# Mixture-of-experts pieces of 32 rows in four column groups, with the results stored from ScalarE

## The chip, the cores and the metric

The kernel runs on one core of one Trainium2 chip. The metric is the device time of one execution in microseconds, the median of several. Times of single instructions, waits and transfers come from one profiled execution of the kernel before.

## The reference, cut to what matters

A backbone of two layers works on 256 latent tokens and 256 context tokens of width 1024. Each layer is normalisation, attention, and then a mixture of 16 experts. In the first layer all 512 tokens go through the experts, in the second only the 256 latent ones. All numbers are float32.

```
def _grouped_moe(t, router_w, router_b, w_gate, w_up, w_down):
    scores = jax.nn.sigmoid((t @ router_w).astype(jnp.float32))
    ...
    g_idx = lax.top_k(grp_score, 1)[1][:, 0]          # one of 4 groups of 4 experts
    ...
    e_idx = lax.top_k(jnp.where(in_group, sel, -jnp.inf), TOP_K)[1]   # the best 2 in it
    ...
    for e in range(N_EXPERTS):
        he = jax.nn.silu(t @ w_gate[e]) * (t @ w_up[e])
        y = y + gates[:, e:e + 1] * (he @ w_down[e]).astype(jnp.float32)
```

Each expert holds three weights of 2 MiB: gate and up (1024 x 512) and down (512 x 1024). Every token gives two rows of work, so a layer has 1024 and 512 rows. The reference's own router, on its inputs of seed 0, gives the experts 0 to 15 these rows:

```
layer 0: 104  81  51  90 | 83  42  83 114 | 55  66  72  49 | 42  28  35  29
layer 1:  22  15  31  18 | 30   4  21  45 | 26  16  22  30 | 70  87  38  37
```

## The kernel before, in words

All engines run programs written out by hand, in order, and meet only at semaphores. `ring` is an SBUF buffer of nine slots of 2 MiB. In the expert stage they are three sets of gate, up and down, and expert 3i + a uses set a. SP issues all weight loads.

The router's results decide at run time how many chunks each expert has. VectorE counts rows per expert, works out each token's position (`posidx`) and each chunk's first row (`chunk_row`). GpSimd (POOL) scatters the tokens' normalised rows into the DRAM tensor `h_rows`, sorted by expert, with indirect DMAs. Then the experts run chunk by chunk: POOL loads a chunk's rows of 1024 numbers, PE turns them (`turn_rows`, L574), ACT copies them out of PSUM to `hc_t` (L802, L803), and PE multiplies them with gate and up (L584, `gate_up`). The result is turned (L601), silu and product are applied by ACT (L810, L814) and VectorE (L1181 to L1193), and PE multiplies with down (L611). ACT copies the result to `yrow` (L818, L820) and POOL stores it to the DRAM tensor `y_rows` (L928). After the last chunk POOL gathers the rows of each token back (L939), and they are added to the stream.

A chunk has up to 128 rows in layer 0, or 64 where an expert's last chunk needs no more, and 64 rows in layer 1. A chunk of 64 rows packs two matmuls into the two halves of the array's columns, with 64 columns each: gate and up side by side, or the two halves of down's output. The numbers of chunks follow from the rows above: layer 0 has 16, eight of 128 and eight of 64 rows, and layer 1 has 18 of 64 rows.

When an expert's last chunk is through, a tiny matmul (L618) raises `set_free`, and SP loads the weights of the expert three places on into that set (L302). Experts 0 to 2 are loaded before the stage. There is one buffer for a chunk's rows: the load of chunk g + 1 starts when chunk g's rows are turned. There is one `yrow`: ACT waits for the stores of the chunk before it.

## Time and profile before

| | before |
|---|---|
| median of 3 runs | 1252.38 us (1247.89 to 1255.44) |
| the profiled execution, its own time | 1254.75 us |
| its span, first to last instruction | 1252.9 us |
| mean granted TensorE clock | 0.916 of full speed |
| PE busy | 1048.7 us (84%) |
| DMA traffic | 317.77 MB, mean 254 GB/s |

PE is TensorE's matmul part and PEld its weight loads. SPq, ACTq and POOLq are the sequencers of those engines, where a DMA's issue shows. A float32 matmul shows as two MATMUL instructions. The DMA share is the mean busy share of the 16 DMA engines, and it can read a little over 1. The expert stage of layer 0 lies at about 410 to 707 us, that of layer 1 at about 947 to 1222 us.

### The profile page before, as it was taken

The numbers are of one execution on the slowest core, as the hardware profiler recorded it, in microseconds if no ns is written. First come the engines' busy times: TensorE is split into PE (matmuls) and PEld (weight loads), VectorE is DVE, ScalarE is ACT, GpSimd is POOL, SyncE is SP. The second block draws the span as 40 slices with busy tenths as digits, with TensorE's granted clock in tenths as the row PEclk, the third lists the DMA queues.
The fourth block names the chain that finished last, engine by engine and source line by source line (L and its number), as shares of the span: only waits on it lengthen the run. The fifth ranks groups of instructions, "written<-read, shape, count | busy, mean of one in ns | idle before, by whom it ended". The sixth has DMA issues, their size and how long they took to land.

```text
span 1252.9 us, 16814 instructions
## 1 busy us (share of the span) xinstructions
PE 1048.7 (84%) x5809; PEld 663.6 (53%) x5810; DVE 383.7 (31%) x1019; ACT 360.1 (29%) x766; POOL 86.9 (7%) x145
## 2 busy tenths in 40 slices
PE   4799989988963899999999459988938987787992
PEld 2244654433443677676755356855835555454652
DVE  1356666563144000000011064778160100000112
ACT  3322255552031122122122143267021221221221
POOL 0000000000002001001011110000010110110111
PEclk9899999998965899999999769999967988888996
DMA  9930299797033189999999980050352999999953
GB/s 318 401 151 0 89 387 329 259 362 272 0 134 134 52 308 400 344 399 346 398 348 397 414 315 1 13 207 1 135 201 88 382 378 380 381 379 388 374 171 109
DMA packets 127534, 317.77 MB, mean 254 GB/s; under 512 B 5872, under 2 KB 6144, under 8 KB 127488
## 3 DMA queue, kind: packets, MB, share of 16 engines
q1 hardware_dynamic: 113680, 276.54, 59.3%
q0 software_dynamic: 12096, 40.38, 9.0%
q8 instruction: 30, 0.49, 0.2%
q10 hardware_dynamic: 1712, 0.23, 0.1%
q14 instruction: 16, 0.13, 0.0%
HBM read 296.68 MB, written 19.40 MB: 252 GB/s over the span
## 4 chain that ended last, share of the span: by engine, by line
PE 65%; SPq 11%; DMA 8%; DVE 7%; ACT 4%; issue 3%; POOL 1%; ACTq 1%; POOLq 0%; DVEq 0%
PE bank L584 17%; SPq L302 11%; PE bank L435 9%; PE bank L611 9%; PE bank L535 7%; DMA ring<-in_w_up_dram 4%; PE bank L378 3%; PE bank L505 3%; PE bank L476 2%; PE bank L574 2%; PE bank L488 2%; PE bank L546 1%; PE bank L444 1%; DVE h_t L1010 1%; PE bank L423 1%
## 5 line engine op out<-in xcount | busy, mean ns | idle before, releaser
L584 PE MATMUL bank<-ring,h_t 128*64 128x256 f32 (+1 forms) x2176 | 317.0, 401 | 31.1 <-DMA ring<-in_w_up_dram 28.3
L584 PEld LDWEIGHTS bank<-ring,h_t 128*64 128x64 f32 (+1 forms) x2176 | 232.3, 157 | 104.1 <-issue 44.0
L611 PE MATMUL bank<-ring,h_t 128*64 128x512 f32 (+1 forms) x544 | 151.8, 597 | 17.2 <-DVE h_t L1193 14.6
L435 PE MATMUL bank<-h_t,ring 128*128 128x512 f32 (+1 forms) x320 | 118.4, 525 | 12.3 <-ACT h_t L719 12.3
L1184 DVE COPY h_t<-bank 128x256 f32<-128x256 f32 x52 | 22.1, 424 | 338.7 <-PE bank L584 338.7
L611 PEld LDWEIGHTS bank<-ring,h_t 128*64 128x64 f32 (+1 forms) x544 | 56.5, 149 | 91.2 <-issue 91.2
L435 PEld LDWEIGHTS bank<-h_t,ring 128*128 128x128 f32 x320 | 62.6, 196 | 60.8 <-issue 41.0
L535 PE MATMUL bank<-tokm,ring 128*128 128x512 f32 (+1 forms) x256 | 85.7, 497 | 1.0 <-DVE tokm L1032 1.0
L574 PE MATMUL bank<-cst,h_t 128*128 128x128 f32 x288 | 40.6, 286 | 38.6 <-DMA h_t<-h_rows 38.6
L991 DVE RECIPROCAL work<-work 128x512 f32<-128x512 f32 (+1 forms) x20 | 54.3, 2713 | 59.5 <-ACT work L729 59.5
L1010 DVE TENSOR_REDUCE h_t<-bank 128x1 f32<-128x512 f32 (+1 forms) x96 | 57.3, 597 | 47.8 <-PE bank L476 26.5
L814 ACT ACTIVATE h_t<-bank 128x128 f32<-128x128 f32 x52 | 12.9, 278 | 201.5 <-PE bank L601 201.5
L535 PEld LDWEIGHTS bank<-tokm,ring 128*128 128x128 f32 x256 | 49.4, 194 | 37.7 <-issue 31.8
L779 ACT ACTIVATE h_t<-bank 128x512 f32<-128x512 f32 (+1 forms) x96 | 50.2, 524 | 57.3 <-PE bank L488 30.1
L768 ACT ACTIVATE ring<-bank,h_t 128x512 f32<-128x512 f32 (+1 forms) x96 | 58.5, 610 | 5.3 <-DVE h_t L1015 4.4
L574 PEld LDWEIGHTS bank<-cst,h_t 128*128 128x128 f32 x288 | 32.9, 145 | 49.6 <-issue 48.8
L818 ACT ACTIVATE work<-bank 128x512 f32<-128x512 f32 x34 | 20.3, 597 | 134.6 <-PE bank L611 134.6
L1181 DVE TENSOR_TENSOR h_t<-bank,h_t 128x256 f32<-128x256 f32 x16 | 6.8, 424 | 168.7 <-ACT h_t L810 168.7
L488 PE MATMUL bank<-cst,ring 128*128 128x128 f32 x320 | 50.6, 280 | 8.0 <-DVE ring L1025 6.7
L928 POOL DMA_DIRECT2D y_rows<-work x68 | 37.0, 543 | 197.7 <-issue 196.2
L488 PEld LDWEIGHTS bank<-cst,ring 128*128 128x128 f32 x320 | 35.3, 141 | 27.2 <-DVE ring L1025 20.3
L476 PE MATMUL bank<-ring 64*128 64x128 f32 (+3 forms) x144 | 47.0, 434 | 1.6 <-DMA work<-ring 1.6
(175 smaller groups left out, 1115.6 us busy)
## 6 DMA issues: line engine op xcount, KB each, us to landing
ring<-in_w_gate_dram SPq DMA_DIRECT2D x32, 2048.0 KB, 16.3
ring<-in_w_up_dram SPq DMA_DIRECT2D x32, 2048.0 KB, 22.3
ring<-in_w_down_dram SPq DMA_DIRECT2D x32, 2048.0 KB, 21.8
ring<-in_ada_w_dram SPq DMA_DIRECT2D x24, 2048.0 KB, 10.4
ring<-in_w_in_dram SPq DMA_DIRECT2D x8, 1536.0 KB, 21.9
h_t<-h_rows POOLq DMA_DIRECT2D x18, 512.0 KB, 7.1
ring<-in_w_out_dram SPq DMA_DIRECT2D x4, 2048.0 KB, 10.5
y_rows<-work POOLq DMA_DIRECT2D x52, 128.0 KB, 5.3
```

Source lines behind the costliest of these rows:

```text
L302: sp.dma_start(slot(s, k), src).then_inc(ew_in[l][s], 16)
L435: last = mm(bank[1 + i % 2][:, 0:widths[i]], qk_weights(i, k), h_t[:, k, 0:widths[i]], start=(k == 0), stop=(k == KD - 1))
L476: last = mm(o[:, c0:c1], q_t, k_t[:, c0:c1], start=True, stop=(c0, c1) != masked)
L488: last = turn(bank[4 + n % 2][:, P * q:P * q + P], probs[:, n % 4, P * q:P * q + P], ident)
L535: last = mm(bank[4 + m % 2][:, 0:P * nt], wout[k // 4][:, k % 4, P * m:P * m + P], y_t[:, k, 0:P * nt], start=(k == 0), stop=(k == KD - 1))
L574: last = turn(bank[5 + k // 4][:, P * (k % 4):P * (k % 4) + P], hc[:, P * k:P * k + P], ident)
L584: last = mm(o, hc_t[:, k, 0:rows], w[s][:, k, 256 * half:256 * half + 256], start=(k == 0), stop=(k == KD - 1))
L611: last = mm(o, he_t[:, k, 0:rows], wd[:, k, 512 * n:512 * n + 512], start=(k == 0), stop=(k == KF - 1))
L768: do(probs[:, n % 4, 0:kn], bank[n % 4][:, 0:kn], ACT.Exp, bias=negmax[:, n:n + 1], scale=SCALE, accum_out=lsum[:, n:n + 1]).then_inc(exp_ ...
L779: do(probs_t[:, 0:nk, col:col + P], bank[4 + n % 2][:, 0:P * nk].rearrange("p (k q) -> p k q", k=nk), ACT.Identity).then_inc(pt_ready, 1)
L991: v.reciprocal(rstd[:, 0:n], rstd[:, 0:n])
L1010: link(v.tensor_reduce(smx[:, n:n + 1], bank[n % 4][:, 0:keys(tt)[1]], AX.X, ALU.max))
```

## The change

The experts work on pieces of 32 rows in both layers, and every expert has at least two pieces (`LEAST`), empty ones included. A piece's matmuls use four column groups of 32: for each of 8 slices of the contraction, four matmuls of 256 columns (gate and up, two halves each), and for each of 4 slices four quarters of down's output. The rows of each expert start at a multiple of 32 in `h_rows` and `y_rows`, with gaps between, so piece g is rows 32g to 32g + 31 and `chunk_row` is gone. SP fills both tensors with zeros (from a block of zeros in `table`) early in the program. A piece is loaded as 128 partitions of 256 numbers, two pieces ahead, into two buffers `hc_got`; VectorE copies it to `hc`, and after PE's two transposes to `hc_t`. The down product of piece g - 1 stands behind gate and up of piece g. ACT itself issues four stores of 32 KB for each piece. Gate and up slots are refilled when the last gate and up product of their expert is done, and the down slot when its last down product is done. In the route step the piece counts now come before `posidx`.

In the diff the removed functions of PE, ACT and POOL are left out where they are shown above; "..." marks every cut.

```diff
-SHORT = P // 2
-CHUNK = [P, SHORT]
-MAXCH = TOK_TILES[0] * P // CHUNK[0]
-MAX_CHUNKS = [NE + 2 * t * P // n for t, n in zip(TOK_TILES, CHUNK)]
-GT = max(MAX_CHUNKS) + 2
-ROWS = 2 * (SEQ + CTX)
+CHUNK = 32
+MAXCH = TOK_TILES[0] * P // CHUNK
+LEAST = [2, 2]
+MAX_CHUNKS = [n * NE + 2 * t * P // CHUNK for n, t in zip(LEAST, TOK_TILES)]
+ROWS = P * -(-CHUNK * (max(MAX_CHUNKS) + 3) // P)
...
+        hc_got = hflat[:, 0:512]
+        hc = hflat[:, 1280:1536]
+        hc_t = hflat[:, 512:768].rearrange("p (k r) -> p k r", k=KD)
+        he = hflat[:, 768:1024]
+        act_g = hflat[:, 1024:1152].rearrange("p (j m) -> p j m", j=2)
+        he_t = hflat[:, 1152:1280].rearrange("p (j m) -> p j m", j=2)
+        pos = work[:, 736:744]
+        yrow = work[:, 0:256]
...
+            def refill(l, e, a):
+                done = end_of(sp, l, e)
+                sp.wait_ge(gu_mm[l], done)
+                load_expert(l, e + 3, a, (0, 1))
+                sp.wait_ge(down_mm[l], done)
+                load_expert(l, e + 3, a, (2,))
...
+                    for rows_dram in (h_rows, y_rows):
+                        sp.dma_start(rows_dram[:, :].rearrange("(n p) d -> p n d", p=P),
+                                     table[:, C_Z:C_ALL].unsqueeze(1).to_broadcast([P, ROWS // P, D])
+                                     ).then_inc(rows_zeroed, 16)
...
-                with sp.Fori(1, 5) as i:
+                sp.wait_ge(route_ready, l + 1)
+                with sp.Fori(0, 4) as i:
                     for a in range(3):
-                        sp.wait_ge(set_free[l][a], i)
-                        load_expert(l, 3 * i + a, a)
-                sp.wait_ge(set_free[l][0], 5)
-                load_expert(l, 15, 0)
+                        refill(l, 3 * i + a, a)
+                refill(l, 12, 0)
...
             def experts(l):
                 def turn_rows(n):
 
...
+                    pe.wait_ge(hc_moved[l], n + 1)
+                    for j in range(2):
+                        last = turn(bank[5][:, P * j:P * j + P], hc[:, P * j:P * j + P], ident)
+                    last.then_inc(hc_turned[l], 1)
+                def gate_up(g, a):
+                    w = [ring[:, 3 * a + s, :].rearrange("p (k n) -> p k n", k=KD) for s in range(2)]
+                    pe.wait_ge(hc_ready[l], g + 1)
                     for k in range(KD):
...
+                        for q in range(4):
+                            last = mm(bank[1][CHUNK * q:CHUNK * q + CHUNK, 0:256], hc_t[:, k, :],
+                                      w[q // 2][:, k, 256 * (q % 2):256 * (q % 2) + 256],
+                                      start=(k == 0), stop=(k == KD - 1))
                     last.then_inc(gu_mm[l], 1)
 
...
+                def turn_he(g):
+                    pe.wait_ge(he_ready[l], g + 1)
+                    for j in range(2):
+                        last = turn(turned_he[:, j, :], he[:, P * j:P * j + P], ident)
+                    last.then_inc(he_turned[l], 1)
+                def down(g, a):
                     wd = ring[:, 3 * a + 2, :].rearrange("p (k n) -> p k n", k=KF)
...
+                    pe.wait_ge(het_ready[l], g + 1)
                     pe.wait_ge(rows_ready[l], g + 1)
                     for k in range(KF):
...
+                        h = he_t[:, k % 2, CHUNK * (k // 2):CHUNK * (k // 2) + CHUNK]
+                        for q in range(4):
+                            last = mm(bank[4][CHUNK * q:CHUNK * q + CHUNK, 0:256], h,
+                                      wd[:, k, 256 * q:256 * q + 256], start=(k == 0), stop=(k == KF - 1))
                     last.then_inc(down_mm[l], 1)
 
...
+                def weights_in(a, turns, parts):
+                    for part in parts:
+                        pe.wait_ge(ew_in[l][3 * a + part], 16 * turns)
+                def expert_long(e, a, turns, prev):
+                    g0, g1 = first_of(pe, l, e), end_of(pe, l, e)
+                    weights_in(a, turns, (0, 1))
+                    gate_up(g0, a)
+                    turn_rows(g0 + 1)
+                    if prev is not None:
+                        down(g0 - 1, prev)
+                    weights_in(a, turns, (2,))
+                    turn_he(g0)
+                    with pe.Fori(g0 + 1, g1) as g:
+                        gate_up(g, a)
+                        turn_rows(g + 1)
+                        down(g - 1, a)
+                        turn_he(g)
...
+                expert = expert_long if LEAST[l] > 1 else expert_short
                 pe.wait_ge(route_ready, l + 1)
                 turn_rows(0)
+                expert(0, 0, 1, None)
                 with pe.Fori(0, 5) as i:
...
+                    expert(3 * i + 1, 1, i + 1, 0)
+                    expert(3 * i + 2, 2, i + 1, 1)
+                    expert(3 * i + 3, 0, i + 2, 2)
+                if LEAST[l] > 1:
+                    down(all_chunks(pe, l) - 1, 0)
...
             def experts(l):
...
+                act.wait_ge(route_ready, l + 1)
+                act.wait_ge(rows_zeroed, 32)
+                with act.Fori(0, all_chunks(act, l)) as g:
+                    act.wait_ge(he_turned[l], g + 1)
+                    do(act_g, turned_he[:, :, 0:2 * CHUNK], ACT.Silu).then_inc(silu_done[l], 1)
                     act.wait_ge(down_mm[l], g + 1)
...
+                    act.wait_ge(rows_stored[l], 64 * g + 64)
+                    do(yrow, bank[4][:, 0:256], ACT.Identity).then_inc(rows_ready[l], 1)
+                    act.wait_ge(rows_ready[l], g + 2)
+                    for q in range(4):
+                        act.dma_start(y_rows[bass.ds(CHUNK * g, CHUNK), 256 * q:256 * q + 256],
+                                      yrow[CHUNK * q:CHUNK * q + CHUNK, :]).then_inc(rows_stored[l], 16)
...
+                def load_rows(n, i):
+                    pool.dma_start(hc_got[:, 256 * i:256 * i + 256],
+                                   h_rows[bass.ds(CHUNK * n, CHUNK), :].rearrange("r (q c) -> (r q) c", q=4)
+                                   ).then_inc(hc_in[l][i], 16)
+                load_rows(0, 0)
+                load_rows(1, 1)
+                total = all_chunks(pool, l)
+                with pool.Fori(0, (total + 1) // 2) as m:
+                    for i in range(2):
+                        pool.wait_ge(hc_moved[l], 2 * m + 1 + i)
+                        load_rows(2 * m + 2 + i, i)
+                pool.wait_ge(hc_in[l][0], (total + 3) // 2 * 16)
+                pool.wait_ge(hc_in[l][1], (total + 3) // 2 * 16)
+                pool.wait_ge(hc_moved[l], total + 2)
+                pool.wait_ge(rows_stored[l], total * 64 + 64)
...
+                link(v.scalar_tensor_tensor(out=cmp3, in0=cst[:, C_G + 1:C_G + MAXCH].unsqueeze(1).to_broadcast([P, NE, MAXCH - 1]),
+                                            scalar=rows, in1=tot.unsqueeze(2).to_broadcast([P, NE, MAXCH - 1]),
+                                            op0=ALU.mult, op1=ALU.is_lt))
+                link(v.tensor_reduce(nch, cmp3, AX.X, ALU.add))
+                link(v.tensor_scalar(nch, nch, float(LEAST[l] - 1), 1.0, ALU.max, ALU.add))
+                link(v.tensor_tensor(tri3, nch.unsqueeze(1).to_broadcast([P, NE + 1, NE]), fe, ALU.mult))
+                link(v.tensor_reduce(firstf, tri3, AX.X, ALU.add))
+                v.tensor_copy(first[:, :], firstf).then_inc(route_ready, 1)
+                link(v.scalar_tensor_tensor(out=te(rank), in0=firstf[:, 0:NE].unsqueeze(1).to_broadcast([P, nt, NE]),
+                                            scalar=rows, in1=te(rank), op0=ALU.mult, op1=ALU.add))
...
+                def rows_turned(n):
+                    dve.wait_ge(hc_turned[l], n + 1)
+                    v.tensor_copy(hc_t.rearrange("p (q j) r -> p j q r", j=2),
+                                  bank[5][:, 0:256].rearrange("p (j r q) -> p j q r", j=2, q=4)).then_inc(hc_ready[l], 1)
+                def rows_in(n):
+                    dve.wait_ge(hc_in[l][0], (n + 2) // 2 * 16)
+                    if not isinstance(n, int) or n > 0:
+                        dve.wait_ge(hc_in[l][1], (n + 1) // 2 * 16)
+                    v.tensor_copy(hc, hc_got[:, bass.ds(n % 2 * 256, 256)]).then_inc(hc_moved[l], 1)
+                rows_in(0)
+                rows_turned(0)
+                rows_in(1)
+                with dve.Fori(0, all_chunks(dve, l)) as g:
+                    dve.wait_ge(gu_mm[l], g + 1)
+                    v.tensor_copy(he, bank[1][:, 0:256]).then_inc(he_ready[l], 1)
+                    rows_turned(g + 1)
+                    dve.wait_ge(silu_done[l], g + 1)
+                    v.tensor_tensor(he_t, act_g, turned_he[:, :, 2 * CHUNK:P], ALU.mult).then_inc(het_ready[l], 1)
+                    rows_in(g + 2)
```

PE, the expert stage of layer 0. Before, one chunk of 64 rows (L584 gate and up, L574 turn the next rows, L601 turn the hidden values, L611 down):

```order
L584 MATMUL bank<-ring,h_t 64x256 [waits ew_in0_4,ew_in0_3]
L584 MATMUL bank<-ring,h_t 64x256 x31
L574 MATMUL bank<-cst,h_t 128x128 [waits hc_in0]
L574 MATMUL bank<-cst,h_t 128x128 x7
...
L601 MATMUL bank<-cst,h_t 128x128 [waits he_ready0]
L601 MATMUL bank<-cst,h_t 128x128
...
L611 MATMUL bank<-ring,h_t 64x512 [waits het_ready0,rows_ready0,ew_in0_5]
L611 MATMUL bank<-ring,h_t 64x512 x3
L611 MATMUL bank<-ring,h_t 64x512 [waits het_ready0]
L611 MATMUL bank<-ring,h_t 64x512 x3
```

Of the change, the loop over the second and later pieces (L572 gate and up, L563 turn rows, L592 down of the piece before, L581 turn the hidden values):

```order
L572 MATMUL bank<-ring,h_t 32x256 [waits hc_ready0]
L572 MATMUL bank<-ring,h_t 32x256 x31
...
L563 MATMUL bank<-cst,h_t 128x128 [waits hc_moved0]
L563 MATMUL bank<-cst,h_t 128x128
L592 MATMUL bank<-ring,h_t 32x256 [waits rows_ready0,het_ready0]
L592 MATMUL bank<-ring,h_t 32x256 x15
L581 MATMUL bank<-cst,h_t 128x128 [waits he_ready0]
L581 MATMUL bank<-cst,h_t 128x128
```

The down product has moved behind the next piece's gate and up, and the turning of the hidden values now comes last.

ACT, the loop body of the expert stage in layer 0. Before, for a chunk of 64 rows (L814 silu, L802 and L803 the next rows, L818 the result):

```order
L814 ACT_TABLE_LOAD
L814 ACTIVATE h_t<-bank 128x128 [waits he_turned0]
...
L802 ACTIVATE h_t<-bank 128x512 [waits hc_turned0]
L803 ACTIVATE h_t<-bank 128x512
...
L817 ISA [waits down_mm0]
L818 ACTIVATE work<-bank 128x512 [waits rows_stored0]
```

Of the change, one piece (L817 silu, L820 the result, L823 the stores):

```order
L817 ACT_TABLE_LOAD
L817 ACTIVATE h_t<-bank 128x128 [waits he_turned0]
L819 ISA [waits down_mm0]
L820 ACTIVATE work<-bank 128x256 [waits rows_stored0]
...
L823 ISA [waits rows_ready0]
L823 DMA y_rows<-work 32x256
L823 ISA
L823 DMA y_rows<-work 32x256
L823 ISA
L823 DMA y_rows<-work 32x256
L823 ISA
L823 DMA y_rows<-work 32x256
```

The copies of the next rows have left ACT for VectorE. Four DMA issues have come, and they stand ahead of the next turn's table load and silu.

## Rows read from the trace of the kernel before

**Rows 1.** The page: DMA share in 40 equal slices of the span, in tenths.
```profile
DMA  9930299797033189999999980050352999999953
```
**Rows 2.** The chain that ended last, layer 0's expert stage: start, duration, what.
```profile
413.26 15.85 PE bank L584 x64
...
666.13 26.08 DMA ring<-in_w_up_dram
692.35 8.81 PE bank L584 x64
703.18 3.67 PE bank L611 x16
```
**Rows 3.** The same chain, layer 1's expert stage.
```profile
947.17 9.88 PE bank L584 x64
...
1143.36 9.08 PE bank L584 x64
...
1218.77 3.67 PE bank L611 x16
```
**Rows 4.** Timeline of SP's issues: the first refill of layer 0 and of layer 1.
```profile
438.23 0.39 SPq L302 DMA_DIRECT2D ring<-in_w_gate_dram  x1
...
963.25 0.38 SPq L302 DMA_DIRECT2D ring<-in_w_gate_dram  x1
```
**Rows 5.** Windows in layer 1, and early in the program; the last three numbers are PEclk, DMA share, GB/s.
```profile
970.00:980.00 10.00, 9.44 (x70) 5.53 (x70) 1.18 (x4) 3.35 (x6) 1.60 (x3) 1.00 1.05 371
1200.00:1210.00 10.00, 9.44 (x70) 5.32 (x67) 1.35 (x4) 1.98 (x5) 1.49 (x3) 1.00 0.35 114
60.00:80.00 20.00, 20.00 (x50) 9.31 (x49) 8.56 (x7) 4.31 (x8) 0.00 (x0) 1.00 0.76 287
80.00:145.00 65.00, 65.00 (x186) 35.05 (x186) 42.19 (x44) 14.33 (x23) 0.00 (x0) 1.00 0.00 0
```
**Rows 6.** Timeline of a 64-row chunk in layer 0: start, duration, what, idle before.
```profile
460.80 7.13 PE L584 MATMUL bank<-ring,h_t 128*64 128x256 f32 x64
467.86 1.10 PE L574 MATMUL bank<-cst,h_t 128*128 128x128 f32 x8
468.79 0.60 PE L601 MATMUL bank<-cst,h_t 128*128 128x128 f32 x4
469.20 0.50 ACT L814 ACTIVATE h_t<-bank 128x128 f32<-128x128 f32 x2 [4.32 <-PE bank L601]
469.52 0.51 DVE L1193 TENSOR_TENSOR h_t<-h_t,bank 128x128 f32<-128x128 f32 x2 [1.12 <-ACT h_t L814]
469.95 3.65 PE L611 MATMUL bank<-ring,h_t 128*64 128x512 f32 x16 [0.56 <-DVE h_t L1193]
```
**Rows 7.** Timeline: matmuls of four column groups of 512 columns, adaLN weights.
```profile
33.50 1.90 PE L378 MATMUL bank<-ring,scv 128*2 128x512 f32 x16
```
**Rows 8.** Timeline, layer 1: ACT copies the result, then loads silu's table.
```profile
1209.49 0.60 ACT L818 ACTIVATE work<-bank 128x512 f32<-128x512 f32 x1 [3.04 <-PE bank L611]
...
1210.11 1.28 ACT L814 ACT_TABLE_LOAD   x1
```
**Rows 9.** Groups by line and form: an ACT copy of 256 columns.
```profile
L810 ACT ACTIVATE h_t<-bank 128x256 f32<-128x256 f32 x14 | 5.4, 384 | 68.7 <-PE bank L584 68.7
```
**Rows 10.** One line each: POOL's stores, POOL's row loads, issue to landing min/median/max.
```profile
DMA to landing us min/median/max: 2.2/5.4/7.6
...
DMA to landing us min/median/max: 3.3/6.6/8.6
```
**Rows 11.** Timeline of ACT's own DMA issues at the program's start.
```profile
2.47 1.09 ACTq L842 DMA_DIRECT2D h_t<-in_c_dram  x1
3.59 0.28 ACTq L842 DMA_DIRECT2D h_t<-in_c_ctx_dram  x1
```
**Rows 12.** The chain between the scatter and the first chunk of layer 0.
```profile
400.19 4.52 DMA h_rows<-tokm,posidx
406.24 3.52 DMA h_t<-h_rows
```

240 lines of the change are left out of this document (42 added, 198 removed).

## The prediction
> **What bounds the kernel now.** I read the page's time slices first. The DMA engines are busy for 80% or more of slices 15 to 24 (438 us on) and 90% or more of 32 to 38 (971 us on), the two expert stages [rows 1]; everything the change does to the steady work lies there. Then the chain. In layer 0 it starts on PE, with the first gate and up product at 413.3 us, and ends on the loads: the last expert's up weight is in flight from 666.1 and lands at 692.2. PE ends the stage at 706.85 (703.18 + 3.67) [rows 2]. So layer 0 is PE's for most of the stage and the loads' at its end. In layer 1 the loads bound the middle. Expert 12's up weight is what PE waits for until 1143.4. From there PE has six chunks of 64 rows to do and ends at 1222.4 [rows 3]. The windows say the same: full DMA share from 970 on, and 0.35 in the window from 1200 [rows 5], so the last weight lands at about 1203. The refills begin at 963.25 [rows 4], which makes (1203 - 963.25) / 13 = 18.5 us for one expert's weights with its rows.
>
> **How many pieces.** Each expert has its rows divided by 32, rounded up, and at least 2. The rows listed above give 42 pieces in layer 0 (4 3 2 3, 3 2 3 4, 2 3 3 2, 2 2 2 2) and 34 in layer 1 (twelve times 2, then 3 3 2 2). A chunk of 64 rows took about 13.1 us of PE (1143.36 to 1222.44 for six, rows 3); two pieces have to be measured against that.
>
> **A piece on PE.** Gate and up took 7.13 us for 64 rows over two column groups. The number of matmuls stays, four run together instead of two: 3.5 us. The down product: 3.65 us becomes 1.8. Two transposes of rows instead of eight in 1.10 us: 0.3. Two of hidden values instead of four in 0.60 us: 0.3 [all rows 6]. That is 5.9, and I take 6.0 for a piece bound by PE. That four column groups run together the trace shows at 512 columns: 16 instructions in 1.90 us [rows 7], where two groups of the same length need 3.65 [rows 6].
>
> The Trainium skill speaks against that: "TensorE: Matmul & The Clock Gate", section "Measured speedup vs the span model": three column tiles gave 2.38x instead of 3x. By it 3.5 + 1.8 us would be 6.7, a piece 7.3 us, and the sum about 1256 us. The row above has no such loss, but it has 512 columns and not 256. A rival below takes it up.
>
> **A piece on ACT.** The order listing shows the loop: silu, wait for the down product, copy the result, four DMA issues, table load, next silu. From the end of the down product of piece g - 1 to that of piece g:
> - PE's semaphore 0.13, the copy of 256 columns 0.38 [rows 9], its semaphore and registers 0.15;
> - four issues. Without company one took 0.28 us, and one took 1.09 [rows 11]; I take 0.42 with its register step: 1.7;
> - loop and branch 0.25, the table load 1.28 [rows 8], silu 0.28, semaphore 0.05, VectorE's product 0.29 (0.51 for two that overlap, rows 6), semaphore 0.1;
> - the down product itself 1.8.
>
> The sum is 6.4 us. It is above PE's 6.0, so ACT, not PE, would set the pace: the silu of a piece stands behind the stores of the one before.
>
> **The store's round trip.** There is one `yrow`. The copy of piece g's result waits until all four stores of piece g - 1 have landed. The last of them is issued 1.8 us after the copy began (0.38 + 0.15 + three issues), so a piece cannot be shorter than about 1.8 us plus its landing. No row shows a store from ACT. The nearest are POOL's, two a chunk, of 128 or 256 KB: 2.2 us at least, 5.4 in the median, 7.6 at most [rows 10]. So a piece takes between 6.4 (landing up to 4.6) and 9.4 us. POOL spends part of its time on making the descriptors, and layer 0's DMA would be slightly less than full; I take 4.9 us, which is nearest to the median, and a piece of 6.7 us.
>
> The page "DMA: Bandwidth & Descriptors", section "Queues, rings and completion order", of the Trainium skill says that each DMA engine goes round between the queues at packet granularity. By it ACT's small stores would wait for one packet of SP's and land near the minimum, which gives pieces of 6.4 us. POOL's median of 5.4 against 2.2 speaks against it.
>
> **Loads of rows.** The load of a piece is issued some two pieces ahead of its use, 13 us, and POOL's loads landed in 3.3 to 8.6 us [rows 10]. Hidden; with one buffer only it would cost up to 2 us a piece. VectorE has four short operations in a piece, under 2 us of 6.7: hidden.
>
> **Layer 0.** The start of the first product moves little. Later come four operations ahead of `posidx`, 0.2 to 0.45 us each, +1.4. Earlier: no register load of `chunk_row` between the scatter's landing at 404.7 and the load at 406.2 [rows 12], -1.2; a load of a quarter of the bytes, two transposes instead of eight and one short copy instead of two long ones, against VectorE's extra copy, -1.5. So the first product starts at 412.0. PE's clock is at half there: 64 rows took 9.88 us where a later chunk took 7.13 [rows 3, 6], so I add 1.9. The end is then 413.9 + 42 x 6.7 = 695.3 us against 706.85: **-11.5 us**. The loads set a floor: first refill at 413.9 + 3 x 6.7 + 3.5 = 437.5, hardly before today's 438.2 [rows 4]. Thirteen experts at 18.5 us end at 678, the last up weight lands some 6 us before, and two pieces and a down product follow it: 686. At 6.4 us a piece this floor binds: -21.
>
> **Layer 1.** The start is 1.3 us earlier as well: 945.9, 947.4 with the slow clock. Gate and up slots come free after the second gate and up product, at 947.4 + 6.7 + 3.5 = 957.6 instead of 963.25. As the loads set the pace until expert 12, its up weight lands 5.7 us earlier, at 1137.7. Then come ten pieces: 1139.7 + 10 x 6.7 = 1206.7. The last up weight at about 1192, two pieces and a down product give 1208. The later one counts: **-14 us**.
>
> **The rest.** The zeros are 17.8 MB. SP reaches them at about 72 us, and between 80 and 145 us the DMA engines do nothing [rows 5]. At the 371 GB/s of a full window [rows 5] they need 48 us: hidden. At half that rate they would end at 168 us and meet the next loads from 145 on; that costs 0 to 5 us, and I take 0. After the last down product four issues of ACT replace POOL's two, no difference that I can price above 1 us.
>
> **Sum.** 1254.75 - 11.5 - 14 = 1229.3 us for the profiled execution. That one lies 2.4 us above the median of the runs shown, so I predict **1227 us**.
>
> **The rivals.** Both layers together (413.9 + 42 P - 706.85, and 1139.7 + 10 P - 1222.4) give 52 P - 375.6 us for P between 7 and 9, so it breaks even at P = 7.2 us a piece. A change of 0.5%, 6.3 us, is about what a measurement of this kernel can tell; that is P = 7.1 and P = 7.35.
> - *The forecast*: P of 6.5 to 7.1, 1216 to 1246 us. For it: both loops on ACT come out there. Chance 0.38.
> - *Stores land early*, P up to 6.5. Then the loads bind both layers: -21 and -15, 1215 us. Even P = 6.0 would give no more. For it: ACT needs no descriptors made by software. Against: POOL's median. Chance 0.25.
> - *No difference*, P of 7.1 to 7.35, by landings of 5.4 us: 1246 to 1259. Chance 0.09.
> - *A fourth column group has to wait* (slower): the two products take 4/3 of 5.3 us, and P is 7.8 on PE: +30, 1282 us. Against: the four groups of rows 7. Chance 0.04. The Trainium skill's figure above is the same in a milder form.
> - *Stores land late* (slower). With one `yrow`, each microsecond over 5.5 costs 42 us in layer 0 and 10 in layer 1, and the chain has no slack. At a landing of 6.2 us P is 8.0: 52 x 8 - 375.6 = +40, 1292 us. It decides from P = 7.35 on. For it: the maximum of 7.6. Against: as PE slows down the queue gets shorter. Chance 0.12.
> - *ACT's issues stand behind SP's* (slower). The up weight of rows 2 took 26 us from issue to landing, so SP's queue is full of work, and one issue of ACT took 1.09 us where the next took 0.28 [rows 11], both soon after SP's first loads. If a store waits for one issue of SP's, P is 10 to 12: +170 in layer 0 and +100 in layer 1 at 11, about 1520 us. For it that one row alone, of a moment when the queues were far from full. Chance 0.12.
>
> **Chances and range.** Faster: 0.38 + 0.25 = 0.63. Same: 0.09. Slower: 0.12 + 0.12 + 0.04 = 0.28. The range reaches down to 1208, the early stores with 7 us for the errors of the start and the zeros. Up it takes in no difference and the late stores to P of 7.5: 1266 us. What is left out is most of the late stores' far part, the blocked issues, the fourth group, and little below: 0.2.
>
> **What would show it.** In the profile after: a gate and up group of 64 instructions in 3.5 us; the time from one piece to the next 6.4 to 7.0 us in layer 0; the wait ahead of the down product named by VectorE's product or by ACT's copy; ACT's wait ahead of the copy ended by the DMA `y_rows<-work` for part of the pieces; SP's first refill of layer 1 at about 957. If ACT's issues show more than 0.6 us each, or the stores land later than 5.5 us, the prediction is wrong on the high side. If the DMA share in layer 0 is full from 440 on and PE waits for weights, it is wrong on the low side.

## The result: slower by 0.8%, and the profile after

The changed kernel took 1260.87 us (median of 9 runs, 1255.25 to 1265.37), the kernel before 1250.1 us (9 runs, 1247.61 to 1255.44). The ratio is 1.0079, 95% interval 1.0056 to 1.0101. The forecast was 1227 us and faster; the range of 1208 to 1266 holds the time. The profiled execution after has a time of its own of 1258.0 and a span of 1256.3 us.

First the page of the changed kernel: the DMA slices that answer to [rows 1], and the groups of the expert loop.

```profile
DMA  9999498887033389896999944041332999999932
...
L1157 DVE TENSOR_TENSOR h_t<-h_t,bank 128x128 f32<-128x128 f32 x76 | 21.9, 288 | 436.9 <-ACT h_t L817 436.9
...
L817 ACT ACT_TABLE_LOAD x76 | 97.5, 1283 | 180.4 <-issue 170.8
L563 PE MATMUL bank<-cst,h_t 128*128 128x128 f32 x156 | 34.6, 304 | 122.2 <-DVE h_t L1147 122.2
...
y_rows<-work ACTq DMA_DIRECT2D x304, 32.0 KB, 4.7
```

76 pieces ran, 42 and 34, as counted. PE idles 122 us over all pieces ahead of L563, the turn of the *next* piece's rows, until VectorE has copied those rows (L1147), an instruction that had no term in the forecast. The chain that ended last shows a whole piece in layer 0 (start, duration, what):

```profile
503.73 0.39 ACT work L820
504.14 0.05 ACTq L823
504.28 0.32 ACTq L823
504.63 0.04 ACTq L823
504.76 0.32 ACTq L823
505.23 0.32 ACTq L823
505.71 0.32 ACTq L823
...
506.35 1.28 ACT L817
507.65 0.29 ACT h_t L817
507.95 0.12 DVE h_t L1157
...
508.44 0.30 DVE h_t L1147
...
508.79 0.44 PE bank L563 x2
509.23 1.91 PE bank L592 x32
...
511.24 0.39 ACT work L820
```

From copy to copy it is 7.51 us. Two thirds of the pieces of both layers take just that, none takes less, and the others take up to 9.8 (the median pitch of ACT's copies is 7.51 in layer 0 and 7.52 in layer 1). Read it as one loop through three engines, ACT, VectorE and PE: the result's copy, four issues at a pitch of 0.48, the table load, silu, VectorE's product, *then the rows copy behind it*, then PE's turn of the rows, and only behind that the down product. Gate and up lie beside this chain. The timeline has them, and the answer to [rows 6]:

```profile
503.88 3.66 PE L572 MATMUL bank<-ring,h_t 128*32 128x256 f32 x64
...
508.79 0.44 PE L563 MATMUL bank<-cst,h_t 128*128 128x128 f32 x2 [1.25 <-DVE h_t L1147]
...
509.15 1.93 PE L592 MATMUL bank<-ring,h_t 128*32 128x256 f32 x32
```

3.66 us where 7.13 stood, 1.93 where 3.65 stood: four column groups run together at 256 columns too. In the kernel before, a chunk of 128 rows shows what the same 64 matmuls take in one group:

```profile
437.89 14.06 PE L584 MATMUL bank<-ring,h_t 128*128 128x256 f32 x64
```

The windows that answer to [rows 5]:

```profile
970.00:980.00 10.00, 8.80 (x144) 4.66 (x138) 2.09 (x6) 1.95 (x3) 0.70 (x2) 1.00 0.70 240
1200.00:1210.00 10.00, 8.07 (x130) 4.44 (x134) 2.78 (x8) 1.94 (x3) 1.09 (x2) 1.00 0.15 49
60.00:80.00 20.00, 20.00 (x51) 9.50 (x50) 10.15 (x10) 4.94 (x9) 0.00 (x0) 1.00 1.03 384
80.00:145.00 65.00, 63.97 (x188) 35.34 (x186) 40.71 (x41) 14.09 (x23) 2.29 (x4) 1.00 0.71 231
```

From 970 us on the DMA share is 0.70 where it was 1.05: in layer 1 too the pieces set the pace now, and PE waits for the up weights 2.9 us in all, where it was 25.3. The zeros are issued at 56 and 64 us and have landed by 129, and nothing waits for them. Where the time went, by the profiled executions: until layer 0's first gate and up product 413.3 became 406.1 (-7.2); layer 0's experts 293.5 became 324.7 (+31.2); from there to layer 1's first product 240.3 became 230.3 (-10.0); layer 1's experts 275.2 became 266.8 (-8.4); the tail 30.5 became 28.4 (-2.1). These give +3.5 against +10.8 in the medians: before's profiled execution lay 4.7 us over its median, after's 2.9 under, so 7.5 us of the five terms are scatter. The -7.2 at the start is partly scatter and partly two stores that the change dropped, as the last experiment shows.

### The profile page after: what moved, and what is told of

Its sections match the earlier page's. It is cut to its first block, busy times and chain, and to the rows that moved or that the text cites. A ratio compares the mean times of both kernels' runs of the same rounds, so it can differ in the third digit from the quotient of the medians.

```text
span 1256.3 us, 26129 instructions
## 1 busy us (share of the span) xinstructions
PE 1002.4 (80%) x10205; PEld 571.0 (45%) x10206; DVE 436.0 (35%) x1168; ACT 384.4 (31%) x777; POOL 71.7 (6%) x116
## 4 chain that ended last, share of the span: by engine, by line
PE 40%; ACT 12%; ACTq 9%; DMA 9%; issue 7%; DVE 6%; SPq 2%; POOL 1%; DVEq 1%; POOLq 0%
PE bank L592 10%; ACTq L823 9%; PE bank L524 7%; ACT L817 6%; DMA y_rows<-work 4%; PE bank L424 3%; PE bank L494 3%; PE bank L367 3%; PE bank L465 3%; ACT work L820 2%; PE bank L563 2%; PE bank L477 2%; DMA ring<-in_w_up_dram 2%; PE bank L572 2%; SPq L280 2%
## 5 line engine op out<-in xcount | busy, mean ns | idle before, releaser
L572 PE MATMUL bank<-ring,h_t 128*32 128x256 f32 x4864 | 282.1, 384 | 12.5 <-issue 6.4
L572 PEld LDWEIGHTS bank<-ring,h_t 128*32 128x32 f32 x4864 | 153.4, 111 | 120.0 <-issue 28.9
L1157 DVE TENSOR_TENSOR h_t<-h_t,bank 128x128 f32<-128x128 f32 x76 | 21.9, 288 | 436.9 <-ACT h_t L817 436.9
L592 PE MATMUL bank<-ring,h_t 128*32 128x256 f32 x2432 | 150.0, 388 | 10.2 <-DVE h_t L1157 10.2
L563 PE MATMUL bank<-cst,h_t 128*128 128x128 f32 x156 | 34.6, 304 | 122.2 <-DVE h_t L1147 122.2
L424 PE MATMUL bank<-h_t,ring 128*128 128x512 f32 (+1 forms) x320 | 117.6, 523 | 12.3 <-ACT h_t L732 12.3
L820 ACT ACTIVATE work<-bank 128x256 f32<-128x256 f32 x76 | 29.2, 384 | 262.3 <-PE bank L592 229.4
L592 PEld LDWEIGHTS bank<-ring,h_t 128*32 128x32 f32 x2432 | 72.1, 111 | 64.0 <-issue 15.2
L563 PEld LDWEIGHTS bank<-cst,h_t 128*128 128x128 f32 x156 | 15.8, 142 | 158.5 <-DVE h_t L1147 119.3
L907 POOL DMA_DIRECT2D h_t<-h_rows x80 | 43.9, 549 | 528.2 <-DVE h_t L1147 520.8
L465 PE MATMUL bank<-work,ring 64*128 64x128 f32 (+3 forms) x144 | 47.6, 439 | 0.0
```

The lines of the kernel that those rows point to most:

```text
L424: last = mm(bank[1 + i % 2][:, 0:widths[i]], qk_weights(i, k), h_t[:, k, 0:widths[i]], start=(k == 0), stop=(k == KD - 1))
L465: last = mm(o[:, c0:c1], q_t, k_t[:, c0:c1], start=True, stop=(c0, c1) != masked)
L563: last = turn(bank[5][:, P * j:P * j + P], hc[:, P * j:P * j + P], ident)
L572: last = mm(bank[1][CHUNK * q:CHUNK * q + CHUNK, 0:256], hc_t[:, k, :], w[q // 2][:, k, 256 * (q % 2):256 * (q % 2) + 256], start=(k == 0) ...
L592: last = mm(bank[4][CHUNK * q:CHUNK * q + CHUNK, 0:256], h, wd[:, k, 256 * q:256 * q + 256], start=(k == 0), stop=(k == KF - 1))
L820: do(yrow, bank[4][:, 0:256], ACT.Identity).then_inc(rows_ready[l], 1)
```

## The experiments

Edits are against the changed kernel unless said. The times, with the chief numbers that were read from each trace (layer 0 and 1: from the first gate and up product to the last down product; pitch: median of ACT's copies in layer 0; wait: what ACT's copy in layer 0 waited for the stores, from the groups by line):

| kernel | us | ratio to before, 95% | layer 0 | layer 1 | pitch | wait |
|---|---|---|---|---|---|---|
| before | 1250.1 | | 293.5 | 275.2 | | |
| changed | 1260.87 | 1.0056 to 1.0101 | 324.7 | 266.8 | 7.51 | 22 |
| rows_first | 1234.8 | 0.9845 to 0.9894 | 310.2 | 259.0 | 7.10 | 87 |
| table_out | 1222.04 | 0.9744 to 0.9791 | 295.5 | 260.3 | 6.87 | 135 |
| two_yrow | 1223.51 | 0.9765 to 0.9808 | 297.4 | 260.2 | 6.1 and 7.6 | 0 |
| quarter_stores | 1185.89 | 0.9456 to 0.9513 | 271.4 | 246.7 | 6.19 | 14 |
| one_store | 1350.42 | 1.0795 to 1.0831 | 373.2 | 312.4 | 9.41 | 182 |
| silu_first | 1195.16 | 0.9554 to 0.9598 | 270.2 | 252.0 | 6.27 | 0 |
| silu_one_buffer | 1216.78 | 0.9691 to 0.9760 | 298.4 | 251.7 | 6.91 | 247 |
| no_lag | 1240.74 | 0.9919 to 0.9952 | 315.7 | 260.0 | 7.10 | 16 |
| no_lag_two | 1240.92 | 0.9907 to 0.9957 | 315.4 | 260.0 | 7.18 | 0 |
| pool_stores | 1595.92 | 1.2723 to 1.2803 | 507.9 | 416.8 | 12.8 | |
| before_refill | 1232.96 | 0.9864 to 0.9897 | 285.3 | 265.5 | | |
| late_refill | 1280.97 | 1.0211 to 1.0267 | 335.7 | 278.1 | 7.52 | |
| silu_late_refill | 1210.63 | 0.9659 to 0.9720 | 278.4 | 261.2 | 6.27 | |
| with_pads | 1262.39 | 1.0076 to 1.0129 | 329.5 | 266.1 | | |

### Is the chain the bound? Four single edits

**rows_first.**

```diff
+                    rows_in(g + 2)
                     dve.wait_ge(silu_done[l], g + 1)
                     v.tensor_tensor(he_t, act_g, ...).then_inc(het_ready[l], 1)
-                    rows_in(g + 2)
```

> VectorE copies the rows of piece g+2 before it waits for piece g's silu, instead of behind the product. Three theories of the 7.51 us that a piece takes in the changed kernel. T1, one serial chain (down, ACT's copy, four store issues, table load, silu, product, rows copy, turn of the rows, down): the rows copy and the turn leave it, 0.85 us, so 6.7 us a piece, layer 0's expert stage from 325 to about 293 us, layer 1's (34 pieces, near its weight traffic) some 8 us shorter, 1220 us in all (1212 to 1232). T2, TensorE itself at four column groups sets the pace: no change, 1258 to 1263. T3, the round trip of the one result buffer (issue to landing 4.7 us, and ACT's 2.3) sets it: no more than 5 us gained.

Measured: 1234.8 us, 26 under the changed kernel. The chain theory has its mark: the shortest pieces now take 6.65 us, 0.86 less. But only some pieces are short, and most of the 15 us that are missing against the expectation are a new wait. The group of ACT's copy in layer 0, of the changed kernel and then of this one:

```profile
L820 ACT ACTIVATE work<-bank 128x256 f32<-128x256 f32 x42 | 16.1, 384 | 144.3 <-PE bank L592 122.2 <-DMA y_rows<-work 22.1
```
```profile
L820 ACT ACTIVATE work<-bank 128x256 f32<-128x256 f32 x42 | 16.1, 383 | 128.4 <-DMA y_rows<-work 87.1 <-PE bank L592 41.3
```

The copy used to wait for the down product; now it waits for the stores of the piece before. The first limit hid a second one just under it.

**table_out.** A silu of one element ahead of ACT's loop; the trace then has one table load ahead of the loop in each layer, two in all, and none in its body.

```diff
+                do(work[0:1, 0:1], eps[0:1, 0:1], ACT.Silu)
                 with act.Fori(0, all_chunks(act, l)) as g:
```

> A silu of one element stands ahead of ACT's loop over the pieces, so that the loop's body no longer begins with a table load of 1.28 us. T1: the load stands on the chain, so a piece falls from 7.51 us to what is next: 6.2 us by the chain alone, 6.5 us by TensorE's own sum (3.66 + 0.44 + 1.93 + 0.44), 6.8 us by the round trip of the result buffer. I take 6.7: 1218 us in all (1208 to 1230). T2: no change. T3: at most 5 us gained.

Measured: 1222.04 us, 4 over the expected 1218 and within its range. The shortest piece takes 6.23 us (7.51 - 1.28), as the chain says, the median piece 6.87, and the wait for the stores is 135 us (below). The load was never needed a second time: the traces show no load ahead of ACT's copies, and silu runs from turn to turn without one here. It stood in the loop because the loop began without silu's table. The Trainium skill ("ScalarE activation tables: per-element evaluation and per-set limits", section "Table sets in the compiler and the runtime") says that table loads are placed per block; the trace agrees, if the body of the loop is a block: entered without silu's table it has a load in each turn, 76 in all, and entered with it none.

```profile
L821 ACT ACTIVATE work<-bank 128x256 f32<-128x256 f32 x42 | 16.1, 384 | 168.0 <-DMA y_rows<-work 135.0 <-PE bank L592 33.0
```

**two_yrow.** `yrow` becomes two buffers with a semaphore each, and ACT's loop takes two pieces a turn.

```diff
-        yrow = work[:, 0:256]
+        yrow = [work[:, 256 * i:256 * i + 256] for i in range(2)]
...
-                with act.Fori(0, all_chunks(act, l)) as g:
+                with act.Fori(0, all_chunks(act, l) // 2) as m:
+                    for i in range(2):
```

> Two result buffers with a count each; ACT's loop runs over pairs of pieces, so that it has one table load for two pieces instead of two. Two effects are in it. T1: the buffer alone is worth 4 to 5 us (the stretched pieces of layer 0), the halved table loads 0.64 us a piece, 27 us in layer 0: 6.9 us a piece on the mean (7.5 and 6.3 in turn), 1226 us in all (1218 to 1236). T2: no change. T3, the round trip sets the pace: it falls to TensorE's 6.5 us in every piece alike, 1215 us.

Measured: 1223.51 us. In layer 0 the pitch alternates, 6.1 and 7.6 us, as the chain with a table load in every second piece says; a round trip would have shortened all pieces alike.

**quarter_stores.** `for q in range(4)` of the stores becomes `range(1)`; three quarters of the result rows are left out.

> Only the first of the four stores of each piece is issued; the other three quarters of the result rows are left out. T1: three issues at a pitch of 0.48 us leave the chain, 1.4 us, so 6.2 to 6.5 us a piece (TensorE's sum is 6.5), 1210 us in all (1200 to 1222). T2: no change. T3: no more than the shorter landing gives, 1250 or more; T4, the traffic of the stores sets it: also below 1215, but the time then is not in ACT's issues.

Measured: 1185.89 us, lower than expected: pieces go down to 6.19 us, which is PE's own sum (gate and up 3.66, down 1.93, and 0.30 for each pair of transposes, most of whose 0.44 lies beside them), not the 6.5 that I had added up. All four results exclude that the column groups set the pace. This one leaves open whether issues, round trip or traffic was worth it; the next two tell. Its layer 1 can't be compared exactly: with three quarters of the rows missing the router there sees other numbers, and the trace has 33 pieces instead of 34, one piece of some 6 us less.

### One big store, or the stores off the chain

**one_store.**

```diff
-                    for q in range(4):
-                        act.dma_start(y_rows[bass.ds(CHUNK * g, CHUNK), 256 * q:256 * q + 256], yrow[CHUNK * q:...
+                    act.dma_start(y_rows[bass.ds(CHUNK * g, CHUNK), :].rearrange("r (q c) -> q r c", q=4), yrow)
```

> The four stores of a piece's result become one of 128 KB with the same bytes and the same rows of 1 KB. It tells apart why leaving three stores out was worth 75 us. T1, the issues: three issues of 0.48 us leave the chain here too, and the buffer's round trip is as much shorter, so 6.2 to 6.4 us a piece as there (6.19), layer 0's stage about 265 us: 1200 us in all (1190 to 1212). T4, the traffic of the stores beside the weights: nothing of it is gone, so no more than 15 us under the changed kernel, 1245 or more.

Measured: 1350.42 us, a plain miss, in the other direction. The timeline of the stretch beside 500 us:

```profile
500.27 0.55 ACTq L822 DMA_DIRECT2D y_rows<-work  x1
...
501.15 1.28 ACT L817 ACT_TABLE_LOAD   x1 [1.05 <-issue]
...
509.30 0.39 ACT L820 ACTIVATE work<-bank 128x256 f32<-128x256 f32 x1 [6.58 <-DMA y_rows<-work]
```

The issue is as cheap as hoped, but the buffer came free 9.0 us after it. The median of layer 0's 27 waits is 9.2 us. With four stores of 32 KB each lands 4.7 us (median, at most 6.0) after its own issue, and the buffer is free 6.4 us after the first issue (median of the 38 waits of silu_one_buffer below). So the same bytes in one store take some 3 us longer, and with one buffer all of it is paid. Why was not tried, but the counts of DMA packets differ, in the changed kernel and then here:

```profile
DMA packets 142097, 329.37 MB, mean 262 GB/s; under 512 B 10320, under 2 KB 20320, under 8 KB 142048
```
```profile
DMA packets 137537, 329.35 MB, mean 244 GB/s; under 512 B 5760, under 2 KB 15760, under 8 KB 137488
```

All 4560 missing packets are small, 60 for each of 76 pieces. The trace has 32 packets of 1 KB and 16 of 4 bytes for a store of 32 KB, and 128 of 1 KB and only 4 of 4 bytes for the store of 128 KB. If each 4-byte packet stands for one DMA engine that took part, the one store went over 4 engines and each small one over 16. That would explain the longer time; it is argued from the counts, not shown.

**silu_first.** The whole traffic, nothing of it in the chain: two buffers as above, `rows_in(g + 2)` first as above, and ACT's loop in another order, with the first silu ahead of it.

```diff
+                silu(1)
+                with act.Fori(0, half - 1) as m:
+                    for i in range(2):
+                        result(down_mm, 2 * m + 1 + i, m + 1, i)
+                        silu(2 * m + 2 + i)
+                        store(2 * m + 1 + i, i)
```

> Two result buffers, the silu of the next piece ahead of the stores in ACT's loop (its first one stands ahead of the loop, and the table load with it), and VectorE's rows copy ahead of its wait for silu. All four stores stay. T1: nothing of ACT is left between two down products but a copy of 0.38 us, so TensorE sets the pace, 6.19 us as with one store of four: layer 0's stage 42 x 6.2 = 260 us, 65 less than in the changed kernel; layer 1 comes down to its weight traffic, some 10 less: 1188 us (1180 to 1200). T4, traffic: no better than 1215.

Measured: 1195.16 us, 4.2% faster than the kernel before (ratio 0.9576). The timeline shows the period that the change could have had:

```profile
505.34 0.38 ACT L827 ACTIVATE work<-bank 128x256 f32<-128x256 f32 x1 [5.76 <-PE bank L593]
505.49 3.66 PE L573 MATMUL bank<-ring,h_t 128*32 128x256 f32 x64
505.62 0.27 ACT L822 ACTIVATE h_t<-bank 128x128 f32<-128x128 f32 x1
505.90 1.80 ACTq L832 DMA_DIRECT2D y_rows<-work  x4
505.92 0.29 DVE L1181 TENSOR_TENSOR h_t<-h_t,bank 128x128 f32<-128x128 f32 x1 [1.78 <-ACT h_t L822]
...
509.45 1.93 PE L593 MATMUL bank<-ring,h_t 128*32 128x256 f32 x32
```

VectorE's product is done at 506.2 and the down product that needs it starts at 509.45, so PE waits for nobody: it is the bound, in layer 0. In layer 1 PE stands between its own pace and the loads': pieces of 6.3 us alternate with waits for weights (what waited, for what: us in all, times, longest).

```profile
PE bank L573 <- DMA ring<-in_w_up_dram: 25.6, 7, 5.4
```

Stores of 32 KB and their traffic cost nothing that layer 0 shows once nothing waits behind them: its stage takes 270.2 us here and 271.4 with three quarters of them gone. In all it is 1195 us against 1186, where one piece less in layer 1 of quarter_stores is most of the 9 us.

**silu_one_buffer.** The same with one `yrow`.

> The fastest version (silu of the next piece ahead of the stores, table load ahead of the loop, rows copy ahead of the wait for silu) with one result buffer, as in the changed kernel. The order alone leaves TensorE's 6.19 us a piece. If the round trip of the one buffer is the second limit, which the growing wait for the stores says (22 us in layer 0 of the changed kernel, 87 with the rows copy moved, 135 with the table load out): copy 0.4, silu 0.3, issues 2.0, landing 4.7 or less from the last issue, about 6.9 us on the mean as with the table load out, 1222 us in all (1214 to 1230). If the wait was only the place where slack of the rest shows: 1197 (1193 to 1202).

Measured: 1216.78 us. The second buffer is worth 22 us, and nearly all of the wait is the stores':

```profile
L826 ACT ACTIVATE work<-bank 128x256 f32<-128x256 f32 x42 | 16.1, 383 | 268.7 <-DMA y_rows<-work 246.6 <-PE bank L592 22.1
```

So the round trip of one buffer is a limit of its own, 6.9 us a piece. My 6.7 us was this limit, 0.2 too small; the chain stood above it.

### The down product one piece later

**no_lag.** PE's order alone: the expert's loop of the changed kernel's other form, in which the down product follows its own piece.

```diff
-                expert = expert_long if LEAST[l] > 1 else expert_short
+                expert = expert_short
...
-                if LEAST[l] > 1:
-                    down(all_chunks(pe, l) - 1, 0)
```

> TensorE's order of one piece undone: the down product follows its own piece's transposes, and is not one piece later. The list for TensorE: gate and up 3.66, turn of the rows 0.44, turn of the product 0.44, then silu 0.28, VectorE's product 0.29 and the steps between them some 0.2, down 1.93: 7.25 us, with the stores and the table load (4.2 us from the end of down) beside gate and up of the next piece. T1: 7.3 us a piece, held up to 7.5 by the result buffer's round trip, so about as long as with the later down, 1254 us (1246 to 1264): the later down bought nothing here. The rival, by which the later down did hide silu and its product: slower by 1 us a piece, 1300 us.

Measured: 1240.74 us, 20 us *faster* than the changed kernel, where I had expected 7, and below the range. The timeline:

```profile
502.64 0.38 ACT L818 ACTIVATE work<-bank 128x256 f32<-128x256 f32 x1 [2.49 <-PE bank L592]
503.19 1.75 ACTq L821 DMA_DIRECT2D y_rows<-work  x4
505.26 1.28 ACT L815 ACT_TABLE_LOAD   x1 [2.24 <-issue]
...
506.49 0.44 PE L581 MATMUL bank<-cst,h_t 128*128 128x128 f32 x2 [0.17 <-DVE h_t L1152]
506.97 0.28 ACT L815 ACTIVATE h_t<-bank 128x128 f32<-128x128 f32 x1 [0.42 <-PE bank L581]
507.28 0.29 DVE L1155 TENSOR_TENSOR h_t<-h_t,bank 128x128 f32<-128x128 f32 x1 [0.49 <-ACT h_t L815]
...
507.67 1.93 PE L592 MATMUL bank<-ring,h_t 128*32 128x256 f32 x32 [0.73 <-issue]
```

Stores and table load (503.19 to 506.54) now lie beside gate and up; what is left between is 7.1 us. Where the expert changes, PE's register work stands ahead of gate and up without cover, in the row below 1.10 us, for a mean of 7.45 us a piece; with the later down product most of it was hidden.

```profile
495.19 3.66 PE L572 MATMUL bank<-ring,h_t 128*32 128x256 f32 x64 [1.10 <-issue]
```

The layer also starts its pipe sooner: its first result is copied 10.3 us after the first product, instead of 12.3.

**no_lag_two.** The same with the two result buffers of two_yrow.

> TensorE's order undone as in the run without the later down product, and the two result buffers as well, so that no piece waits for the stores. Does the later down product win anything once ACT's stores are off the chain? T1: without it a piece is TensorE's serial list with the bubbles for silu and product, 7.1 us as measured in the free pieces of that run, now in all pieces, so some 5 us under its 1241 in layer 0 and little in layer 1 (which stands near its weight traffic): 1234 us (1228 to 1240). With the later down product and ACT's order mended a piece was 6.19 to 6.27 us and 1195 us in all: so the later product is worth 40 us there, and cost 20 us where the stores stood in its chain. The rival, that the later down product is worth nothing and the ACT order did it all: 1200.

Measured: 1240.92 us, no difference from no_lag, though the 16 us of waiting for the stores are gone: they had lain beside PE's chain. The free piece stays at 7.0 to 7.2 us. So with ACT's order mended the later down product is worth some 45 us (1195 against 1241), and with the stores in its chain it costs 20. The 45 are argued in part: no run has PE's order undone and ACT's mended. But in the rows above silu starts 0.04 us after the turn of the product ends, so ACT's order isn't what PE waits for there. The rival of no worth is out.

### Who issues the stores

**pool_stores.** The four stores move from ACT's loop to POOL's, behind `load_rows`, and behind a wait for the result.

```diff
                         load_rows(2 * m + 2 + i, i)
+                        pool.wait_ge(rows_ready[l], 2 * m + 2 + i)
+                        for q in range(4):
+                            pool.dma_start(y_rows[bass.ds(2 * CHUNK * m + CHUNK * i, CHUNK), 256 * q:256 * q + 256], ...
```

> The stores of the changed kernel are issued by GpSimd again, behind its row load. T1: four issues leave ACT's chain (2 us), but there is still one result buffer, and its round trip becomes copy 0.4, a row load's issue 0.5, four issues 2.2, landing 5.3 or more: 8.4 us or more a piece, where it stood at 7.5. Layer 0's stage 42 x 8.5 = 357 us, layer 1's 290: 1315 us in all (1290 to 1340). The rival, that ACT's issue time is all that matters: 6.3 us a piece, 1200.

Measured: 1595.92 us, 335 us over the changed kernel where 54 were expected. The round trip was not what did it:

```profile
505.44 2.25 POOL L920 DMA_DIRECT2D y_rows<-work  x4 [10.62 <-ACT work L824]
508.21 0.56 POOL L907 DMA_DIRECT2D h_t<-h_rows  x1 [0.52 <-issue]
513.34 0.29 DVE L1151 COPY h_t<-h_t 128x256 f32 x1 [8.02 <-DMA h_t<-h_rows]
513.69 0.69 PE L563 MATMUL bank<-cst,h_t 128*128 128x128 f32 x2 [5.47 <-DVE h_t L1151]
...
514.31 3.62 PE L592 MATMUL bank<-ring,h_t 128*32 128x256 f32 x32
```

POOL waits 10.6 us for a result, and the row load that the next result needs stands behind that wait in its queue: load, copy, turn, down product, result, stores, load: 13.7 us from this result to the next, 12.8 in the median. PE idles between and its clock falls: the down product takes 3.62 us instead of 1.93 (granted clock 0.53 from 514.3 to 518.0 and 0.74 from 500 to 514, where the changed kernel has 0.99 over its layer 0). The run prices my order of POOL's work, not stores by POOL as such; what it shows is what stands in the queue behind a moved wait.

### The refill by parts, and the pads

**before_refill.** The kernel before with this one part of the change: `refill` waits for `gu_mm` and loads gate and up, then for `down_mm` and loads down; `set_free` and its tiny matmul are gone.

> The kernel before with one part of the change: gate and up weights are refilled as soon as their expert's last gate/up product is done, down weights after its last down product, instead of the three after it. In the kernel before the weights of L0 and L1 start late by a down product and the ones product (some 5 to 8 us an expert, where the queue is not full). If this refill is what won layer 1 its 8.5 us: faster by 6 to 8 us, 1243 us (1238 to 1250). If layer 1's gain came from the pieces: no change, 1250.

Measured: 1232.96 us, 15.4 us less than its own runs of before, twice the expectation: 8.2 us in layer 0 and 9.7 us in layer 1 by the profiles. These two lie 27 us apart, 12 more than the medians, so the split is rough. Layer 1's first refill is issued 9.7 us after the first product (941.07 against 931.4), not 16.1 [rows 4].

**late_refill.** The same part undone in the changed kernel.

```diff
-                sp.wait_ge(gu_mm[l], done)
-                load_expert(l, e + 3, a, (0, 1))
                 sp.wait_ge(down_mm[l], done)
-                load_expert(l, e + 3, a, (2,))
+                load_expert(l, e + 3, a)
```

> The changed kernel with the refill by parts undone: an expert's gate and up weights are loaded over only when its last down product is done, which in this order is one piece after its last gate and up. With 7.5 us a piece layer 0 needs 325 us for weights that take some 254, so it hides there: 0 to 4. Layer 1 (34 pieces, 267 us) stands near its traffic: each refill starts 5.6 us later, and where the ring is the bound it is paid: 8 to 20 us. In all 1272 (1262 to 1285). If the refill by parts brought layer 1's gain, most of the 8.5 us that layer 1 was shorter than in the kernel before come back here; if not, 1261.

Measured: 1280.97 us, 20 us more than the changed kernel, where 11 were expected: 11 in each layer by the profile. In layer 1 PE's waits for `in_w_up` grow from 2.9 to 11.1 us; in layer 0 no wait for weights is named, so that half is not explained by a row (its window from 440 to 500 us has a granted clock of 0.91). Some of it may be scatter: layer 0 takes 329.5 us in with_pads, whose expert stage is that of the changed kernel with 324.7.

**silu_late_refill.** The same undone in the fastest version.

> The fastest version with all three weights of an expert loaded over only after its last down product. In the changed kernel that cost 20 us, half of it in each layer. With pieces of 6.2 us TensorE asks for the weights faster (layer 0's 42 pieces in 260 us, the traffic some 250), so late refills are paid in both layers: 20 us or more again, 1220 us (1212 to 1235). The rival, that the refill matters only beside slow pieces: 1200 or less.

Measured: 1210.63 us, 15.5 more than silu_first and just under the range. The refill is worth 15 to 20 us at each of the three paces tried.

**with_pads.** The kernel before stores two pads of 512 KB of zeros behind `h_rows` and `y_rows` at its start. The change drops them, and its description doesn't name that. Here they and ACT's wait for them are put back.

> The changed kernel with the two stores of 512 KB of zeros and ACT's wait for them put back, as in the kernel before. The first stretch of the changed kernel's profile was 3.6 us shorter than that of before. If that is the stores' doing: 1264.5 us (1262.5 to 1266). If it is scatter between profiled executions: 1261.

Measured: 1262.39 us, 1.5 over the changed kernel with intervals that overlap: the time alone shows no effect. The traces show one. PE's first instruction, in the changed kernel and then here:

```profile
11.30 0.39 PE L660 MATMUL bank<-cst,h_t 96*128 96x96 f32 x1 [11.30 <-DMA h_t<-in_table_dram]
```
```profile
14.63 0.40 PE L662 MATMUL bank<-cst,h_t 96*128 96x96 f32 x1 [14.63 <-DMA h_t<-in_table_dram]
```

PE starts at 14.6 to 14.9 us in the three profiles with the pads (before, before_refill, with_pads) and at 11.3 to 11.7 in the 13 without. Layer 0's first product stands at 407.0, 407.4 and 413.3 us with them, and at 401.9 to 407.1 without. So of the 7.2 us by which the changed kernel's profile started layer 0 earlier, some 3 are the pads' and the rest is scatter. Whether they reach the total, 1.5 us can't tell.

## Why the prediction was wrong

I forecast 23 us less than before and measured 11 us more. **The step that failed** is the one of the loads of rows: "VectorE has four short operations in a piece, under 2 us of 6.7: hidden". The sum of an engine's work was small; its place was not. The rows copy stands behind VectorE's wait for silu, the turn of the rows that needs it stands ahead of the down product on PE, and so both joined the chain that I had listed under "a piece on ACT". That list gave 6.4 us; the trace has 7.51, 0.85 of it the rows copy with its registers and the turn, the rest small terms (four issues to the table load 2.07 us from the first issue's start, where I had 1.7 + 0.25; down 1.93 against 1.8). Moving the copy alone took 0.86 us from the free pieces and 26 us from the kernel. The forecast's own formula, 52 P - 375.6, gives +15 us at P = 7.51. That the range holds the time is luck: its upper part stood there for stores that land late, and they landed as taken.

**Right:** the number of pieces; gate and up 3.66 (3.5 forecast) and down 1.93 (1.8); ACT's loop above PE, with the table load in it; the landing of ACT's stores (4.7 us, 4.9 taken); that a round trip of the one buffer is a limit near there (6.9 us by silu_one_buffer, 6.7 taken); the hidden zeros; the sign of each rival: the fourth group does not wait, ACT's issues of 0.32 us do not stand behind SP's (three of 304 took over 1 us, the longest 1.79), the stores do not land late, nor near their least of 1.5 us.

**Layer 0:** -11.5 forecast, +24 at its end (706.85 became 730.87), which is 42 pieces at 0.8 us more than taken, 34 us. **Layer 1:** -14 forecast, its stage -8.4: with pieces of 7.5 us the formula gives -7.6. That agreement is luck in part: the formula lets the loads set the pace up to expert 12, and in this profile the pieces do it throughout, with 2.9 us of waits for the up weights. The refill gave the gain: its first issue stood 10.8 us after the first product (971.97) instead of 16.1, and late_refill gives 11 us of layer 1 back. **The start:** -1.3 forecast, with no term for the dropped pads, and -7.2 in the profiles. **Between the layers** I had priced nothing and the profile has -10.0. All kernels with the change's pieces take 230 to 237 us there, where before takes 240.3 and before_refill 238.6. Which part of the change shortens it was not tried. The pace of layer 0 does not settle it: 237.1 us follow the 270.2 of silu_first, but 235.6 follow the 507.9 of pool_stores.

**The parts of the change, as the runs price them:** refill by parts -15 (in the kernel before) and -20 (in the changed one); the later down product +20 as made, about -45 with ACT's order mended; one result buffer instead of two +22 in the mended version; the rows copy's place +26; the table load in the loop +39 (which is not additive with the rows copy, since the round trip catches both). Pieces, column groups and refill were good for 1217 us with the one buffer and 1195 us with a second; the places of silu, the table load and the rows copy made it 1261.

## What to carry to other kernels

Moving a product one step later doesn't take a chain away, it picks another one: write out, for each engine and in program order, what stands ahead of the next down product, with the waits of *other* engines' instructions that stand behind it, and add that up around the loop. An engine that is 35% busy can still hold the loop, by one 0.3 us copy behind the wrong wait. Stores belong behind whatever the next step waits for, and where a loop's first function has its table not loaded on the way in, the loop pays the load every turn: one instance of the function ahead of the loop took 1.28 us from the shortest pieces. When one limit is lifted, look at what the same instruction waits for next (here 22, 87, 135, 247 us for the stores) before the gain is promised.

## What the runs showed of the hardware that was not expected

- One store of 128 KB over 128 partitions freed its buffer 9.2 us after its issue (median), four of 32 KB 6.4 us after the first issue, with the same packets of 1 KB. The one has 4 small packets of 4 bytes, the four have 64.
- ACT's four issues cost 0.32 us each at a pitch of 0.48, beside a DMA share of 0.85 to 0.93 in layer 0; their landing was 1.5 to 6.0 us.
- Four column groups of 32 rows run 64 matmuls of 256 columns in 3.66 us, against 7.13 for the same number over two groups of 64 and 14.06 in one of 128: hardly a loss from the fourth group. The Trainium skill's 2.38x for three column tiles ("TensorE: Matmul & The Clock Gate", section "Measured speedup vs the span model") does not hold for this shape: going from two groups to four gave 1.95x (7.13 / 3.66), and from one to four 3.84x.
- In pool_stores the same 32 down matmuls took 3.62 us instead of 1.93, which is the clock's lower level (1.2 instead of 2.4 GHz; granted 0.53 from 514.3 to 518.0), after PE had waited 5.5 us for the rows copy.
